# Six gate products move from a merge stage into a recurrence, and the merge takes its projections in two passes

## The reference

```python
h = rms_norm(x, pre_mix_g)
proj = h @ w_in                       # attention, rwkv and gate columns
y_a = chunk_band_attention(...)       # 512 columns
y_b = rwkv7_time_mix(...)             # 512 columns, a delta rule over time
gate_a = sigmoid(p_gate[..., :1024])
gate_b = sigmoid(p_gate[..., 1024:])
merged = gate_a * (y_a @ proj_a) + gate_b * (y_b @ proj_b)
x = x + rms_norm(merged @ w_out, post_mix_g)
```

## Time and profile before

| | before |
|---|---|
| median of 3 runs | 2206.53 us (2203.7 to 2212.47) |
| span of the profiled execution | 2203.0 us |
| PE busy | 2159.4 us, 98% of the span |
| DVE, ACT, POOL busy | 931.9, 876.8, 889.5 us |
| chunks, from the first pair products to the norm's means | 287.76 to 453.15 us |
| merge, from there to the first product with `w_out` | 453.15 to 541.94 us |

### The profile page before, as it was taken

One profiled execution on the slowest core, in us unless ns is written; L12 is line 12 of the kernel. 1 busy time (PEld: TensorE's weight loads), 2 busy tenths in 40 slices (PEclk: granted clock), 3 DMA queues, 4 the chain that ended last, 5 costly groups with the idle time before them and its releaser, 6 DMA issues.

```text
span 2203.0 us, 30785 instructions
## 1 busy us (share of the span) xinstructions
PE 2159.4 (98%) x12606; PEld 1753.4 (80%) x12614; DVE 931.9 (42%) x1580; ACT 876.8 (40%) x1647; POOL 889.5 (40%) x686
## 2 busy tenths in 40 slices
PE   8999988999999999999999999999999999999998
PEld 6767778888888888878777888888887678888887
DVE  5231766634441021136325654443237765444322
ACT  4344631134443233234335454443235435444322
POOL 4523400025344444554222354444444345444443
PEclk9999988999999999999999999999999999999998
DMA  7222200014223323222111122223322122233321
GB/s 270 87 73 91 71 17 2 3 48 144 77 96 101 100 89 103 96 67 87 58 49 58 58 77 96 96 96 105 96 67 92 52 77 77 97 98 101 98 96 58
DMA packets 53013, 183.05 MB, mean 83 GB/s; under 512 B 5752, under 2 KB 5760, under 8 KB 52744
## 3 DMA queue, kind: packets, MB, share of 16 engines
q1 hardware_dynamic: 52872, 181.08, 25.3%
HBM read 176.32 MB, written 7.62 MB: 83 GB/s over the span
## 4 chain that ended last, share of the span: by engine, by line
PE 94%; DVE 3%; DMA 1%; ACT 1%; POOL 1%; issue 1%; SPq 0%; POOLq 0%; DVEq 0%; ACTq 0%
PE ps L329 22%; PE ps L331 21%; PE ps L330 21%; PE ps L1562 3%; PE ps L2583 2%; PE ps L2585 2%; PE ps L2584 2%; PE ps L355 2%; PE ps L349 1%; PE ps L350 1%; PE ps L1092 1%; DMA raw_units<-stream 1%; PE ps L461 1%; PE ps L1094 1%; PE ps L467 1%; PE ps L1093 1%
## 5 line engine op out<-in xcount | busy, mean ns | idle before, releaser
L184 POOL TENSOR_TENSOR split_units<-raw_units,split_units 128x512 fp32r<-128x512 f32 x628 | 818.8, 1329 | 1254.7 <-ACT split_units L174 1254.6
L174 ACT ACTIVATE split_units<-raw_units 128x512 fp32r<-128x512 f32 x628 | 359.1, 621 | 366.5 <-PE ps L331 333.5
L329 PE MATMUL ps<-x_split,split_units 128*128 128x512 f32 x1224 | 481.5, 393 | 1.7 <-DVE work L2243 0.8
L330 PE MATMUL ps<-x_split,split_units 128*128 128x512 f32 x1224 | 477.0, 390 | 0.0
L331 PE MATMUL ps<-x_split,split_units 128*128 128x512 f32 x1224 | 476.9, 390 | 0.0
L329 PEld LDWEIGHTS ps<-x_split,split_units 128*128 128x128 f32 x1224 | 230.1, 188 | 55.1 <-issue 4.0
L330 PEld LDWEIGHTS ps<-x_split,split_units 128*128 128x128 f32 x1224 | 230.3, 188 | 48.9 <-issue 1.7
L331 PEld LDWEIGHTS ps<-x_split,split_units 128*128 128x128 f32 x1224 | 230.2, 188 | 47.9
L329 PE MATMUL ps<-hidden_split,split_units 128*128 128x512 f32 x608 | 237.3, 390 | 0.0
L331 PE MATMUL ps<-hidden_split,split_units 128*128 128x512 f32 x608 | 236.6, 389 | 0.0
L330 PE MATMUL ps<-hidden_split,split_units 128*128 128x512 f32 x608 | 236.5, 389 | 0.0
(11 more groups left out here) (475 smaller groups left out, 3263.1 us busy)
## 6 DMA issues: line engine op xcount, KB each, us to landing
raw_units<-stream SPq DMA_DIRECT2D x314, 512.0 KB, 3.7
bias_rows<-bias_line SPq DMA_DIRECT2D x1, 2816.0 KB
gate_rows<-work SPq DMA_DIRECT2D x10, 256.0 KB, 2.1
work<-gate_rows SPq DMA_DIRECT2D x10, 256.0 KB, 2.8
x<-x_t SPq DMA_DIRECT2D x4, 512.0 KB, 6.5
work<-bias_rows SPq DMA_DIRECT2D x1, 2048.0 KB
out_t<-x SPq DMA_DIRECT2D x8, 256.0 KB
vec<-vectors SPq DMA_DIRECT2D x1, 1159.5 KB, 8.3
```

The costliest lines, as they stand in the source:

```text
L174: scalar.activation(self.split[:, u % SPLIT, 0, part], self.raw[:, u % RING, part], ACT.Copy).then_inc(self.high_done, 1)
L184: gpsimd.tensor_tensor(self.split[:, u % SPLIT, 1, part], self.raw[:, u % RING, part], self.split[:, u % SPLIT, 0, part].bitcast(F32), ALU ...
L329: TE.matmul(out, high, rhs(0, k), start=(k == 0), stop=False)
L330: TE.matmul(out, high, rhs(1, k), start=False, stop=False)
```

## The change

Gate tiles m = 0..2 (six units) are no longer computed in the merge. They are computed on PE among the turns and level steps of the chunks: two in each of chunks 0 and 1, one in each of chunks 2 and 3. In a chunk 6 dense matmuls stand after the first turn and 5 after the second, the rest is spread over the first 25 of the 29 level steps. ACT copies the result to a new tile `staged` and rounds the next weight unit; SP writes it to `gate_rows`, which now has 16 tiles. The merge loads all 16 back, applies all sigmoids from there, and takes first the eight `y_a` halves (each multiplied by its gate at once, `first_gated`, into eight tiles `w[:, MG + m]`), then the eight `y_b` halves. DVE makes the low parts of `y_a` before it centres `y_b`. The weight stream is put in that order (that part of the diff, and the closing of semaphore counts, are left out below).

```diff
+CHUNK_GATES = tuple((m, j) for m in range(3) for j in range(2))
+GATE_ROWS = EARLY_GATES + CHUNK_GATES
...
+            GATES_BY = ((0, 1), (2, 3), (4,), (5,))
+            FILLED_BY = 6 * (LAST - 1) - 5
+            AT_TURNS = (6, 11)
...
+                def gate_products(b):
+                    out = bank(gate_bank(b))
+                    for k in range(KD):
+                        high, low = wts.take(pe)
+                        TE.matmul(out, high, xs[:, 0, k, :], start=(k == 0), stop=False)
+                        yield
+                        TE.matmul(out, high, xs[:, 1, k, :], start=False, stop=False)
+                        yield
+                        ins = TE.matmul(out, low, xs[:, 0, k, :], start=False, stop=(k == KD - 1))
...
+                        yield
+
+                def products_beside(ch):
+                    for b in GATES_BY[ch]:
+                        wait_dve(pe, gate_group(b), ch, DVE_U)
+                        yield from gate_products(b)
...
+                    def dense_after_step():
+                        nonlocal step
+                        step += 1
+                        dense(min(n_beside, AT_TURNS[1] + (n_beside - AT_TURNS[1]) * step // FILLED_BY))
+
+                    turn(0, ch)
+                    dense(AT_TURNS[0])
+                    turn(1, ch)
+                    dense(AT_TURNS[1])
                     for l in range(1, LAST):
                         level_x(l)(0, ch)
+                        dense_after_step()
                         if l > 1:
                             level_u(l - 1)(1, ch)
+                            dense_after_step()
                         level_x(l)(1, ch)
+                        dense_after_step()
...
+                    for b in GATES_BY[ch]:
+                        pe.wait_ge(read_act.sem, read_act.at(b + 1))
...
+                    for b in GATES_BY[ch]:
+                        stage_gate(b)
+                        wts.round_high(act, S, u0 + b + SPLIT)
...
             def _(pe):
+                def gated_half(m):
+                    if m >= 4:
+                        pe.wait_ge(side_dve.sem, side_dve.at(m - 3))
+                    split_product(pe, bank(m % 4), KH, part(4), tile_ready, m + 1)
+
                 norm_mean(pe)
...
+                pe.wait_ge(norm_low.sem, norm_low.at(4))
+                gated_half(0)
+                gated_half(1)
+                norm_sums(pe)
+                gated_half(2)
+                gated_half(3)
+                norm_spread(pe)
+                for m in range(4, KD):
+                    gated_half(m)
+                pe.wait_ge(norm_low.sem, norm_low.at(KD))
+                for m in range(KD):
+                    if m >= 4:
+                        pe.wait_ge(dve_out.sem, dve_out.at(m - 3))
+                    split_product(pe, bank(4 + m % 4), KH, part(0), tile_ready, KD + m + 1)
...
             def _(sp):
...
+                for n, (m, j) in enumerate(slots):
+                    at = GATE_ROWS.index((m, j))
+                    if n >= 4:
+                        wts.load(sp, u0 + (n - 4) // 2 + RING)
+                        last, before = slots[n - 4]
+                        if before:
+                            sp.wait_ge(var_out.sem, var_out.at(last + 1))
+                        else:
+                            sp.wait_ge(side_dve.sem, side_dve.at(last + 1))
+                    sp.wait_ge(spilled[at % 4], 16 * (at // 4 + 1))
+                    sp.dma_start(w[:, GA + n % 4, :], gate_rows[at]).then_inc(gate_landed[n % 4], 16)
                 wts.load(sp)
...
+                for n in range(4, KD):
+                    sigmoid(n)
+                wts.round_high(act, S, u0 + 3 + SPLIT)
+                for m in range(KD):
+                    sigmoid(KD + m)
+                    wts.round_high(act, S, u0 + 4 + m // 2 + SPLIT)
+                    act.wait_ge(var_out.sem, var_out.at(m + 1))
+                    S.activation(merged_split[:, 0, m, :], w[:, MG + m, :], ACT.Copy).then_inc(high_out.sem, 1)
...
+                first_gated(0)
+                first_gated(1)
...
+                first_gated(2)
...
+                first_gated(3)
...
+                for m in range(4, KD):
+                    first_gated(m)
                 for m in range(KD):
...
+                    gb, mg = w[:, GA + m % 4, :], w[:, MG + m, :]
+                    dve.wait_ge(tile_ready.sem, tile_ready.at(KD + m + 1))
+                    dve.wait_ge(read_act.sem, read_act.at(KD + m + 1))
+                    V.tensor_tensor(gb, bank(4 + m % 4), gb, ALU.mult).then_inc(dve_out.sem, 1)
+                    dve.wait_ge(dve_out.sem, dve_out.at(m + 1))
+                    dve.wait_ge(side_dve.sem, side_dve.at(m + 1))
+                    V.tensor_tensor(mg, mg, gb, ALU.add).then_inc(var_out.sem, 1)
```

More of the change, by code:

```diff
@@ L71 @@
              ("level0_t", HD), ("ident64", HD), ("mask4", 512), ("diag_qk", 128), ("diag_st", 128), ("inv_count", 64), ("eps", 3)]
-def merge_order():
-    order = [("gate", 0)]
-    for m in range(KD):
-        order += [("gate", m + 1)] if m + 1 < KD else []
-        order += [("projection", m)]
-    return order
 def columns(spec):
@@ L246, in network @@
         col = sb("col", [P, 128])
+        staged = sb("staged", [P, 2, T])
         ident_h = sb("ident_h", [P, P], BF16)
@@ L1908, in norm_spread @@
                     ins.then_inc(norm_pe.sem, 1)
-            def norm_wait(pe):
-                pe.wait_ge(norm_low.sem, norm_low.at(KD))
-            between = {1: norm_sums, 2: norm_spread, 4: norm_wait}
             u0 = wts.block // UNIT
@@ L3326, in network @@
             ("merge", stage_merge),
-            ("w_out", lambda: stage_linear(KD, of(merged_split), "copy", wt(0), sums="squares", prior=read_act)),
+            ("w_out", lambda: stage_linear(KD, of(merged_split), "copy", wt(0), sums="squares", prior=side_dve)),
             ("up_a", lambda: stage_relu2_up(post_mix_pre_ffn())),
@@ L3364, in weight_stream @@
     parts = [head[:12].reshape(-1, P, P)] + [gates[j, m] for m, j in EARLY_GATES] + [head[[12 + m for m in RWKV_ORDER]].reshape(-1, P, P)]
-    for kind, m in merge_order():
-        parts += ([gates[j, m] for j in range(2) if (m, j) not in EARLY_GATES] if kind == "gate"
-                  else [pa[m], pb[m]])
+    parts += [gates[j, m] for m, j in CHUNK_GATES] + [pa.reshape(-1, P, P), pb.reshape(-1, P, P)]
     up, down, half = a["w_up"][0], a["w_down"][0], FF1 // 2 * P
```

136 lines of the change are left out of this document (66 added, 70 removed).

## The result

| | before | after |
|---|---|---|
| median | 2205.17 us (2203.7 to 2212.47) | 2228.92 us (2224.14 to 2241.31) |
| ratio of the medians | | 1.0111, interval 1.009 to 1.0132 |
| span of the profiled execution | 2203.0 us | 2231.0 us |
| turns and levels of the four chunks (first turn to first `right_side` matmul), summed | 82.97 us | 126.84 us |
| what follows in each chunk up to the next token turn or the norm's means, summed | 61.40 us | 67.34 us |

The changed kernel is 1.1% slower, 2229 us where 2226 was forecast.

The account below looks back on a forecast made before the run. PE's own time was taken as the bound. -32.6 + 0.7 + 47.7 - 5.1 + 8.8 = +19.5 us gave a span of 2222.5 and a median of 2226 us; own range 2215 to 2235, 8 in 10 for 2197 to 2238.

Parts of the forecast that it names:

- Out of the merge: Merge: 144 gate matmuls at 0.2267 us leave PE's dense stream there, -32.6 us.
- Into the chunks: Turns and levels: moved matmuls cost 0.7 us at the turns and 47.7 in the levels, with 5.1 gained by the clock.
- the price of a change: Levels: each dense group between narrow 64x64 steps costs 0.36 us beyond its matmuls; bounds 0 to 0.36.
- the band: Band stage, where narrow groups of other shapes stand between dense matmuls; its trace gave 0.36 us a group.
- The split: Levels: 0.15 us before a dense group, 0.33 to 0.43 for a single matmul, 0.34 and 0.33 for a pair.
- The first rival: Levels: changing between 64x64 and dense has no price, 22.2 us there; -6.7 in all, 2200 us; chance 18%.
- break-even: Levels: price per dense group at which the change neither gains nor loses, other terms kept: 0.08 us.
- The clock: Levels of chunks 1 to 3: filled pauses at the turns keep the upper clock, -5.1 us; range 0 to 5.1.
- the rival in which the clock falls anyway: Levels: narrow steps with changes leave PE less busy, no 5.1 gain, perhaps 10 us slower work; 2231 to 2241; 6%.
- The end of the merge: Second pass of the merge: PE waits for late weight units and DVE's slices, +8.8 us; bounds 0 and 12.
- the rivals in which the merge keeps up: Merge without stall: with no price for changing, -15.5, 2191 us, 10%; with the band's price, +10.7, 2217 us, 14%.
- The sum: Whole kernel: all terms together +19.5 us, span 2222.5, median 3.5 above it, 2226 us.

Follow-up runs that it names:

- the three numbers of groups: Changed kernel with its 74 dense groups in the levels, or the same matmuls in 24 or 4 groups: 2228.92, 2215.66 and 2204.76 us.
- the kernel with both mends: Changed kernel with the merge's weight units loaded ahead and DVE's low part of slice m-1 put behind the sum of slice m: 2218.09 us, ratio 1.0067.
- the block version with the mends: Changed kernel with level matmuls in one block behind step 2, merge weight units loaded ahead, DVE's low parts one slice later: 2191.56 us, ratio 0.9945.

## Why the prediction was right

**Out of the merge, -32.6.** The stretch to the end of the product with `w_out` is 18.8 us shorter. With 8.1 us of waits, about 2.6 at the lower clock behind two of them (13 matmuls, 0.20 more each), and about 1.5 around the norm (its sums take 4.56 us instead of 3.49, and two or three dense matmuls more behind them take 0.43), -32.6 comes to -20.4; 1.6 us are left without a row. One reading was wrong without harm: at 487.54 only four of the six gate tiles are done, and of the 240 matmuls up to 541.94 in the kernel before 48 are still gate matmuls and 192 the projections'. The 0.2267 us a matmul holds for both.

**Into the chunks, +43.3 (0.7 + 47.7 - 5.1).** Turn to right side is 16.9, 15.0, 6.0 and 6.0 us longer, +43.9. The bold step was to take the price of a change, 0.36, from the band, where other shapes stand between the dense matmuls; it measured 0.34 to 0.35, and the three numbers of groups show it to be a price of the group. The split was right too: 0.14 before, 0.43 for a single (0.33 to 0.43 had been the bounds), 0.33 and 0.33 for a pair. The first rival is out: its 0.08 break-even is far under the price. That the price is for the shape, as I argued with the Trainium skill, TensorEngine Tiling (Array Packing), Key Properties, is half of it. The runs agree with that page for plain float32, where only the shape changes (0.33 us a group); they also show nearly the same where the tiling mode stays and only the format changes (0.28), which the page doesn't tell. For this kernel the forecast is the same either way, since both change at once; for a mend it isn't: giving the dense matmuls the tile shape of the steps would take only 0.06 off the 0.34 us a group.

**The clock, -5.1.** Its step held in the levels (1.00 in all four, so the rival in which the clock falls anyway is out there) and failed by its end: "The low clock late in each chunk is left as it is" is wrong. In this execution the remainders are 5.9 us longer, and nothing is left of the term. The runs don't show that it is always so: with filled turns they show 1.5 to 6.0 us given back of 5.0, so the term should have been about -1, between -3.5 and +1, and -5.1 lay outside. The row for it was there: chunk 0 of the kernel before has the fast levels and the long remainder behind them. In the sum this is the larger of the two errors.

**The end of the merge, +8.8.** PE waits 8.1 us, so the rivals in which the merge keeps up are out. The total is right and its parts are not: the weight units' waits measured 4.4 us (in the sum 1.6), the slices' 3.7 (in the sum 7.2). Of the 4.4, 1.34 (in the sum 0.3) is a unit that lands after 4.8 us, not 3.6, because four gate tiles and two units are started within 3 us; 2.85 (in the sum 1.3) is the first unit of `w_out`, started at 559.03 behind a wait for a sum and landed 3.9 us later. PE begins the product with `w_out` 62.9 us behind the norm's means, where the working put it at 57.8, and slice 7 comes at 73.3, where it was put at 69.8: both late, PE more so, and what PE is late by it needn't wait for. The contention was there: 1.57 and 0.98 us instead of 0.69, beside POOL. (By the Trainium skill, SBUF, Who interferes with whom, a VectorE instruction with two SBUF inputs contends with a GpSimd one that reads SBUF; the trace agrees, with 1.57 against 0.69 us.) Not foreseen: the 2.6 us at the lower clock behind two of the waits.

**The sum.** On the spans +28.0 was measured, +19.5 predicted: 8.5 us too few, of which 5.9 are the clock given back, 5.0 the merge, 0.6 turns and levels, and -3.0 lie in unchanged code. The median came within 3 us of the forecast (2228.9 against 2226), and that is partly luck: the working put the median 3.5 us above the span of the profiled execution, and for the kernel after it lies 2.1 below.

## What to carry to other kernels

Small matmuls and dense ones can share PE, but count how often PE goes from one to the other, not how many dense ones there are: here a group costs 0.34 us beyond its work, more than the matmul in it (0.227). Put the dense ones in as few blocks as the banks and pauses allow. And before a faster clock in one stretch is booked as a gain, look at what the next stretch runs at, in more than one execution.

## What the runs showed of the hardware

- Going from plain float32 to the rounded format and back, at one tile shape, costs 0.28 us; from 64x64 to 128x128 weights and back, at one format, 0.33; both at once 0.34.
- A plain matmul of 256 columns takes two records of 0.21 to 0.22 us, 0.43 in all, where a rounded one of 512 columns takes 0.227.
- Eleven dense matmuls at the pauses of a chunk lift the granted clock of the levels from 0.84 or 0.90 to 1.00. The 15 us behind them then mostly fall from 0.77 to 0.68 (16.2 us instead of 14.8, in 24 of 33 chunks), though PE isn't idle in them; in seven they stay at 14.8 us, in two they take 17.7.
- In the kernel after, PE's waits of 2.85 and 1.88 us in the dense stream of the merge are followed by some 3 us at the lower clock, those of 1.34, 0.20 and 1.79 us are not. The length alone doesn't decide it: waits of 1.36 and 0.96 us in the kernel with both mends are followed by 3 us at the lower clock, the same two of 1.33 and 0.97 us in the block version with the mends by none.
- Of two weight units of 512 KB that SP starts together with four gate tiles of 256 KB, the first lands after 4.8 us and the second after 6.1; one started 11 us later lands after 3.7.
